# Routed experts taken by size in four lanes, two tables between parts of the shared expert, and the router as paired 64-column products

## The reference, cut to what matters

```python
scores = jax.nn.sigmoid((uf @ w_router).astype(jnp.float32))       # 512 tokens x 64 experts
choice = scores + router_bias.astype(jnp.float32)
...
_, top_e = lax.top_k(masked, TOP_K)                                # 8 experts of each token
wts = wts / jnp.sum(wts, axis=-1, keepdims=True) * ROUTED_SCALE
...
hid = jax.nn.silu(xb @ we_gate[e]) * (xb @ we_up[e])               # 1024 -> 256, twice
return (hid @ we_down[e]) * ws[:, None]                            # 256 -> 1024
...
shared = (jax.nn.silu(uf @ ws_gate) * (uf @ ws_up)) @ ws_down
return (routed + shared).reshape(Bsz, S, D)
```

## Time and profile before

| | us |
|---|---|
| median of the three runs | 2282.85 |
| lowest, highest | 2280.35, 2285.98 |
| the profiled execution, its own time | 2279.11 |
| its span in the trace | 2277.0 |
| routed experts: first product of block 0 to first product of block 47 | 1637.25 to 2232.43 |

### The profile page before, as it was taken

The page is one execution under the profiler, slowest core; times in us unless marked ns, Lnnn a source line. Parts: engine busy times, 40 slices in busy tenths (PEclk is TensorE's granted clock), DMA queues, the critical chain, the costliest instruction groups (busy, mean ns, idle before and its releaser), DMA issues.

```text
span 2277.0 us, 31363 instructions
## 1 busy us (share of the span) xinstructions
PE 2165.5 (95%) x11892; PEld 1561.1 (69%) x11893; DVE 1188.7 (52%) x1772; ACT 720.2 (32%) x1121; POOL 714.3 (31%) x444
## 2 busy tenths in 40 slices
PE   7999999999999999999999999999999999988995
PEld 5867567788778766777777778876555555555553
DVE  6566654998871447789888563245411211211112
ACT  4335654333332343433443345123111111111112
POOL 4331023443353323333333326431122222222220
PEclk9999899999999999999999999999999999999998
DMA  4220132455532223222222213321888889989854
GB/s 160 86 81 2 65 112 74 148 187 182 196 128 95 72 77 93 85 64 75 75 69 62 74 56 111 115 94 74 310 255 286 290 275 322 355 291 375 274 174 127
DMA packets 160062, 344.29 MB, mean 151 GB/s; under 512 B 11457, under 2 KB 100545, under 8 KB 141921
## 3 DMA queue, kind: packets, MB, share of 16 engines
q1 hardware_dynamic: 142496, 297.71, 37.1%
q0 software_dynamic: 15232, 39.02, 7.0%
q10 hardware_dynamic: 2240, 6.29, 0.7%
HBM read 326.19 MB, written 33.55 MB: 158 GB/s over the span
## 4 chain that ended last, share of the span: by engine, by line
PE 81%; DVE 7%; DMA 6%; ACT 2%; issue 2%; SPq 0%; POOL 0%; ACTq 0%; DVEq 0%; POOLq 0%
PE bank L884 24%; PE bank L1566 13%; PE bank L1270 9%; PE bank L1587 7%; PE bank L1191 5%; PE bank L1361 3%; PE bank L875 2%; DMA arena<-in_we_gate 2%; DMA arena<-in_we_down 2%; PE bank L1010 1%; PE bank L1368 1%; DMA arena<-in_w_up 1%; PE bank L893 1%; PE bank L1545 1%; PE bank L1047 1%
## 5 line engine op out<-in xcount | busy, mean ns | idle before, releaser
L1566 PE MATMUL bank<-arena,hn 128*64 128x256 f32 x3072 | 346.4, 384 | 17.5 <-DMA arena<-in_we_gate 15.4
L1566 PEld LDWEIGHTS bank<-arena,hn 128*64 128x64 f32 x3072 | 233.0, 139 | 143.5 <-issue 46.7
L784 POOL TENSOR_TENSOR w_low_flat<-arena,in_high 128x1024 fp32r<-128x1024 f32 (+1 forms) x73 | 186.0, 2569 | 337.1 <-ACT in_high L1892 337.0
L2802 DVE TENSOR_TENSOR inv<-inv,bank 128x256 f32<-128x256 f32 x48 | 20.2, 421 | 332.3 <-PE bank L1566 332.3
L1587 PE MATMUL bank<-arena 128*64 128x512 f32 x768 | 175.4, 598 | 8.0 <-DVE arena L2807 7.9
L1270 PE MATMUL bank<-in_x,in_high 128*128 128x512 f32 x384 | 154.7, 403 | 0.0
L762 POOL TENSOR_TENSOR w_low<-arena,w_high 128x2048 fp32r<-128x2048 f32 x22 | 103.1, 4688 | 161.7 <-ACT w_high L1802 161.7
L1270 PE MATMUL bank<-in_x,w_low_flat 128*128 128x512 f32 x384 | 151.3, 394 | 0.0
L1270 PE MATMUL bank<-x_low,in_high 128*128 128x512 f32 x384 | 151.0, 393 | 0.0
L2814 DVE SCALAR_TENSOR_TENSOR sq<-bank,arena 128x512 f32<-128x512 f32 x96 | 72.1, 751 | 147.8 <-PE bank L1587 145.6
L884 PE MATMUL bank<-x_high,w_high 128*128 128x512 f32 x336 | 133.5, 397 | 1.9 <-POOL w_low L762 1.9
(11 more groups left out here) (479 smaller groups left out, 4883.8 us busy)
## 6 DMA issues: line engine op xcount, KB each, us to landing
arena<-in_we_gate SPq DMA_DIRECT2D x47, 1024.0 KB
arena<-in_we_up SPq DMA_DIRECT2D x47, 1024.0 KB
arena<-in_we_down SPq DMA_DIRECT2D x47, 1024.0 KB
arena<-in_w_in SPq DMA_DIRECT2D x38, 1024.0 KB, 5.4
arena<-in_w_ada SPq DMA_DIRECT2D x12, 2048.0 KB, 8.1
arena<-in_w_up SPq DMA_DIRECT2D x22, 1024.0 KB, 10.8
arena<-in_w_in SPq DMA_DIRECT2D x17, 512.0 KB, 5.2
arena<-in_w_out SPq DMA_DIRECT2D x4, 2048.0 KB, 10.6
```

The costliest lines, as they stand in the source:

```text
L784: pool_eng.tensor_tensor(in2_tile(j, "low"), in2_tile(j, "whole"), in2_tile(j, "high").bitcast(f32), ALU.subtract).then_inc(S("w_low"), 1)
L1566: ins = nc.tensor.matmul(rows_of(banks[2 + part][:, 0:FE], c), columns_of(moe["xT"][:, p, :], k, c), moe["gu"][:, 2 * p + c, at:at + FE], ...
```

## The change

There are four edits.

1. **Router as pairs.** Each of the 8 products of 512 columns becomes two of 256 columns, which write partitions 0 to 63 and 64 to 127 of the same bank. The sigmoid then works on 128x256 instead of 64x512, and two transposes of 128x128 take the place of four.
2. **Experts by size.** Each expert gets the key 64 x halves - number. DVE makes a 64x64 matrix of "has a larger key" times halves, and PE sums it (`ranks`), which gives each expert's start `bstart` with the largest first. The running sum falls away. The expert of a place is found by two comparisons and a product with the numbers 0 to 63. Lanes 0, 1, 2, 3 take fourths 0, 3, 1, 2, so that even blocks pair the largest experts with the smallest.
3. **Tables between the shared expert's parts.** `shared_up(1)` is cut by `ranks`, `shared_down` is cut into residual and halves, and the order of PE's program changes: the first two tables stand ahead of the shared expert's tile 2, the other two between tiles 2 and 3.
4. **The end.** `last_h` runs one tile further ahead, and `last_inverse` stands before `last_out`.

```diff
-                ins = nc.tensor.matmul(banks[0][0:E, :], w[:, k, :], hn[:, k, :], start=k == 0, stop=k == KD - 1)
+                for half in range(2):
+                    ins = nc.tensor.matmul(banks[0][E * half:E * half + E, 0:T // 2], w[:, k, :],
+                                           hn[:, k, T // 2 * half:T // 2 * (half + 1)], start=k == 0, stop=k == KD - 1)
...
-                    if tt == 2 and f == 0:
+                    if tt == 3 and f == 0:
...
+            def ranks():
+
+                pe.wait_ge(S("keys_made"), 1)
+                nc.tensor.matmul(banks[3][:, (TT + 2) * E:(TT + 3) * E], ones[0:E, :], pcol("order")[0:E, 0:E], start=True,
+                                 stop=True).then_inc(S("pe_made"), 1)
...
-            shared_up(1)
+            shared_up(1, 0, 4)
+            ranks()
+            shared_up(1, 4, KD)
+            shared_transposes(0)
+            shared_residual(0)
             run_counts()
-            shared_transposes(0)
+            shared_down(0, 0)
             plan_in_rows()
-            shared_down(0)
+            shared_down(0, 1)
+            shared_transposes(1)
+            shared_residual(1)
+            shared_down(1)
             shared_up(2)
-            shared_transposes(1)
-            shared_down(1)
             shared_up(3)
-            for tt in range(TT):
+            for tt in (0, 1):
                 table(tt)
+            shared_transposes(2)
+            shared_residual(2)
+            shared_down(2)
             for tt in (2, 3):
-                shared_transposes(tt)
-                shared_down(tt)
+                table(tt)
+            shared_transposes(3)
+            shared_residual(3)
+            shared_down(3)
...
+            step(nc.vector.scalar_tensor_tensor(pcol("quarter"), pcol("back"), pcol("key"), pcol("quarter"), ALU.mult, ALU.add))
...
-            step(nc.vector.tensor_tensor_scan(moe["bend"], ones[:, 0:E], moe["nb"], 0.0, ALU.mult, ALU.add))
-            step(nc.vector.tensor_tensor(pcol("bstart"), moe["bend"], moe["nb"], ALU.subtract))
+            keys, own = moe["bend"], pcol("junk")
+            step(nc.vector.scalar_tensor_tensor(keys, moe["nb"], float(E), iota[:, 0:E], ALU.mult, ALU.subtract))
+            for name, of in (("own_key", keys), ("own_halves", moe["nb"])):
+                step(nc.vector.tensor_tensor_reduce(out=own[0:E, :], in0=of[0:E, :], in1=ident[0:E, 0:E], scale=1.0, scalar=0.0,
+                                                    op0=ALU.mult, op1=ALU.add, accum_out=pcol(name)[0:E, :]))
+            nc.vector.tensor_scalar(pcol("order")[0:E, 0:E], keys[0:E, :], pcol("own_key")[0:E, :], pcol("own_halves")[0:E, :],
+                                    ALU.is_lt, ALU.mult).then_inc(S("keys_made"), 1)
...
-            for name, at in (("expert", "half"), ("last", "back")):
-                step(nc.vector.tensor_scalar(pcol("junk"), moe["bend"], pcol(at), None, ALU.is_le, ALU.add,
-                                             accum_out=pcol(name)))
-            for name in ("expert", "last"):
-                step(nc.vector.tensor_scalar(pcol(name), pcol(name), float(E - 1), None, ALU.min))
+            inside = (("expert", "half", pcol("junk")), ("last", "back", pcol("order")[:, 0:E]))
+            for _, at, found in inside:
+                counted_step(nc.vector.tensor_scalar(found, pcol("bstart"), pcol(at), None, ALU.is_le))
+            steps_done()
+            for _, at, found in inside:
+                counted_step(nc.vector.scalar_tensor_tensor(found, moe["bend"], pcol(at), found, ALU.is_gt, ALU.mult))
+            steps_done()
+            for name, _, found in inside:
+                counted_step(nc.vector.tensor_tensor_reduce(out=found, in0=found, in1=iota[:, 0:E], scale=1.0, scalar=0.0,
+                                                            op0=ALU.mult, op1=ALU.add, accum_out=pcol(name)))
...
             last_h(0)
+            last_h(1)
             last_inverse(0)
             for tt in range(TT):
-                if tt + 1 < TT:
-                    last_h(tt + 1)
-                last_out(tt)
+                if tt + 2 < TT:
+                    last_h(tt + 2)
                 if tt + 1 < TT:
                     last_inverse(tt + 1)
+                last_out(tt)
```

More of the change, by code:

```diff
@@ L284, in two_blocks @@
         PLAN_COLS, _ = places([(name, 1) for name in ("lane", "pos", "free", "pairs", "minus", "half", "back", "expert", "last",
-                                                      "new", "first", "needed", "key", "fourth", "fourths", "runs")] +
+                                                      "new", "first", "needed", "key", "fourth", "fourths", "runs", "quarter",
+                                                      "own_key", "own_halves")] +
                               [("bstart", E), ("junk", E), ("order", P), ("in1", TT * TOP), ("in2", TT * TOP),
@@ L331, in two_blocks @@
                                                           "tok_done", "g2_row", "scores", "sc_done"))}
-        PE_MADE = {name: n + 1 for n, name in enumerate(("tok_ready", "g2_spread", "sc_ready", "counted", "runs_counted",
+        PE_MADE = {name: n + 1 for n, name in enumerate(("tok_ready", "g2_spread", "sc_ready", "counted", "ranked", "runs_counted",
                                                          "plan_in_rows"))}
@@ L1421, in score_transposes @@
                 pe.wait_ge(S("act_made"), ACT_MADE["scores"])
-                for tt in range(TT):
-                    ins = nc.tensor.transpose(banks[2][:, tt * E:(tt + 1) * E], SCORES_T[:, tt * P:(tt + 1) * P],
-                                              ident[0:E, 0:E])
+                for q in range(TT // 2):
+                    ins = nc.tensor.transpose(banks[2][:, q * P:(q + 1) * P], SCORES_T[:, q * P:(q + 1) * P], ident)
                 ins.then_inc(S("pe_made"), 1)
@@ L1436, in row_transposes, with shared_up @@
                     ins.then_inc(S("ut_ready"), 1)
-            def shared_up(tt):
+            def shared_up(tt, k0=0, k1=KD):
                 if tt >= 2:
                     pe.wait_ge(S("sh_up"), tt - 1)
-                product(banks[tt % 2][:, :], lambda k: hn[:, k, tt * P:(tt + 1) * P], lambda k: moe["sgu"][:, k, :],
-                        KD).then_inc(S("sh_gu"), 1)
+                for k in range(k0, k1):
+                    ins = nc.tensor.matmul(banks[tt % 2][:, :], hn[:, k, tt * P:(tt + 1) * P], moe["sgu"][:, k, :],
+                                           start=k == 0, stop=k == KD - 1)
+                if k1 == KD:
+                    ins.then_inc(S("sh_gu"), 1)
             def shared_transposes(tt):
@@ L1467, in shared_down @@
                                          h[:, 4 * half + q, tt * P:(tt + 1) * P], ident, start=q == 0, stop=False)
+            def shared_down(tt, *halves):
                 pe.wait_ge(S("sh_hT"), tt + 1)
                 pe.wait_ge(S("down_gated"), 2)
-                for half in range(2):
+                for half in halves or range(2):
                     for k in range(2):
@@ L2084, in _ @@
             act.wait_ge(S("product"), PRODUCTS["router"] + 1)
[L2085 removed]
+            nc.scalar.activation(SCORES_T, banks[0][:, 0:T // 2], ACT.Sigmoid).then_inc(S("act_made"), 1)
             def row_tiles(tt):
@@ L2099, in _ @@
             act.wait_ge(S("ch_done"), 1)
-            nc.scalar.activation(moe["sc"], banks[2][:, 0:TT * E].rearrange("p (t e) -> p t e", e=E), ACT.Copy)\
+            nc.scalar.activation(moe["sc"].rearrange("p (h q) e -> p h q e", h=2), SCORES, ACT.Copy)\
               .then_inc(S("act_made"), 1)
```

37 lines of the change are left out of this document (22 added, 15 removed).

## The result

The median is 2263.62 us (2261.2 to 2269.35, 4 runs) against 2282.26 us before, a ratio of 0.992 with a 95% interval of 0.9897 to 0.9943. Measured again, the same code took 2264.25 us against 2280.58 (0.9929, 0.9914 to 0.9945). The main cause is an edit that the text ahead of the prediction does not list.

The account below looks back on a forecast made before the run. PE, busy 95% of the span, was taken as the bound, with late gate weights stalling the loop. Terms -3.8 + 2.0 - 6.1 + 0.5 = -7.4 us took 2282.85 to 2275.4 us, range 2265 to 2283.

Parts of the forecast that it names:

- The sum of -7.4 us: Whole kernel: -3.8 for block 0's earlier start, +2.0 for its slow clock, -6.1 in the loop, +0.5 at the end.
- The router: Router on PE: paired 256-column products run side by side, so it ends at 1562.9 and not 1566.45, -3.6 us.
- The serial rival: Router: the products of a pair run one after the other; sum about -4, 2279 us; chance 0.07.
- stretch of low clock: PE around the router: TensorE granted 0.50 until about 1562, covering 6 of the 8 steps at 0.86 us.
- Edit 2 on DVE and the tables: Ahead of block 0: about +2.5 us on DVE, covered; last table 1.2 us earlier; block 0 starts 3.8 us earlier, router included.
- Block 0: First loop block: new idle stretches ahead of it slow its products, charged +2.0 us (0 to 2.8).
- The loop: Blocks 0 to 47: two stalls of 8.3 us, at 16/17 and 40/41, 16.6 in place of 22.7, -6.1 us.
- The extra load of block 44: Late in the loop: expert 0 loaded for no rows, behind a block without loads, at no cost; about 8 in a pair.
- most of it is not seen: Loop: stalls stay near 22 because fuller early blocks put 128-row gathers beside loads; -1.3 us, some 2282; chance 0.2.
- the clean loop: Loop: less traffic beside 16/17 and 40/41, both stalls fall to 2 us or less; -20, 2263 us; chance 0.1.
- the slower rival: Loop: two-load blocks 8, 24, 29 and 32 stall beside single loads too; +21, 2303 us; chance 0.05.
- The end: Behind the loop: `last_h(1)` delays `last_inverse(0)` by 1.1 us, partly won back; +0.5 us (-0.6 to +1.2).

Follow-up runs that it names:

- second profile of after: The changed kernel measured and profiled once more, same code: 2264.25 us, 0.9929 of the kernel before; span 2261.5 us.
- kernel with the filling products alone: Kernel before with only the PARTS line changed, moving two slices of a state-space filling product from a group's second step to its first: 2275.11 us, 0.9975.
- run with the old order: Changed kernel with PE's old program order behind the router (only `ranks` kept between the halves of `shared_up(1)`) and the old end: 2267.02 us, 0.9934.
- number order: Changed kernel with the key cut to the expert's number, so experts are taken by number in the new lanes: 2278.17 us, 0.9991.

## Why the prediction was wrong

**The step that failed is the list of the parts.** The text ahead of the prediction says that there are four edits, and the prediction costs four. There are five. The fifth is worth 7.5 us of the stage in every trace that has it. The sum of -7.4 us holds for the four: with these alone the time falls by 6.5 us, 0.9971 (0.9961 to 0.9981). It is not a wrong price but a missing term. I looked for what can be late in the last third of the trace only, and called PE "busy 95% of the span" where 8 waits of up to 0.85 us stood in the middle, each behind filling products that the diff touches.

**The router: right in size, -3.6 forecast, -3.3 and -3.4 measured.** Pairs do run side by side: 6.65 us in place of 9.62, and 5.1 to 6.6 in eight traces with pairs, against 9.1 to 9.9 in five without. The serial rival falls. The stage from its first product on shows only 3.0 us of it, and from line 956 to the transposes of the rows it is even less, 12.4 us before and 10.3 now, since the 2.07 us of that line took 1.16 before. But a cut at the router misleads, because stretches of low clock stand in different places in the two traces. "To rows" in the table begins ahead of all of them: 268.8 to 269.0 us in the five traces without pairs, 265.4 to 265.6 in six with them, and 264.2 in two. The timeline of PE 54 us ahead of the router, and the stretch behind that wait (us, busy time, clock, DMA share, GB/s), before:

```profile
1502.70 0.47 PE L893 MATMUL bank<-mixed_high,late_w_high 128*128 128x512 f32 x1 [2.61 <-ACT mixed_high L2072]
...
1503.00:1507.00 4.00, 4.00 (x13) 2.86 (x12) 4.00 (x1) 3.20 (x7) 3.71 (x1) 0.62 0.95 296
...
1553.99 1.16 PE L954 MATMUL bank<-shp,small 128*128 128x128 f32 x8 [0.64 <-DVE small L2208]
```

The same place in the second profile of after:

```profile
1494.57 0.47 PE L895 MATMUL bank<-mixed_high,late_w_high 128*128 128x512 f32 x1 [2.61 <-ACT mixed_high L2096]
...
1495.00:1499.00 4.00, 4.00 (x18) 2.54 (x17) 4.00 (x1) 3.07 (x6) 3.59 (x1) 1.00 0.99 300
...
1544.57 2.08 PE L956 MATMUL bank<-shp,small 128*128 128x128 f32 x8 [0.64 <-DVE small L2232]
```

Before, the clock fell behind the wait of 2.61 us. After, it did not fall behind the same wait, and the way up to the line ahead of the router is 1.3 us shorter for it. Then it fell sooner ahead of the router, which costs about as much again. The kernel with the filling products alone has both halves of this without any pairs: 1.3 us less up to line 954, 1.3 more from there to the transposes (13.7 us), and 268.9 in all. The forecast held the stretch of low clock fixed, up to 1562, and it isn't fixed: that the price comes so near is in part luck, as the two traces with 264.2 show, in which the same router gave 4.8 us. In the second profile of after the clock is at 0.51 from 1544 us on, 4.3 us ahead of the router, and in the kernel before it is still 0.90 in the 4 us that end 0.8 us ahead of it. The granted clock there (us, busy time, clock, DMA share, GB/s), before:

```profile
1552.00:1556.00 4.00, 2.51 (x21) 2.23 (x20) 0.99 (x3) 1.27 (x4) 1.23 (x1) 0.90 0.00 0
1556.00:1560.00 4.00, 3.17 (x4) 0.98 (x5) 4.00 (x7) 4.00 (x7) 3.44 (x2) 0.50 0.00 0
```

The second profile of after:

```profile
1544.00:1548.00 4.00, 2.08 (x8) 1.78 (x8) 1.49 (x3) 1.74 (x4) 2.65 (x2) 0.51 0.00 0
1548.00:1552.00 4.00, 3.67 (x18) 2.31 (x20) 4.00 (x8) 4.00 (x7) 2.03 (x1) 0.50 0.00 0
```

**Edit 2 on DVE and the tables: right in sum.** "I take nothing" for DVE's longer plan holds, because the new order covers it. Without this order the stage is 1.8 us longer than before. The cut for `ranks` costs 0.6 us where I took 0.1, and the old wait of 0.6 ahead of `plan_in_rows` is gone. Table 0 starts 46.4 us behind the transposes of the rows (1607.50 less 1561.07), as before (1612.87 less 1566.38, 46.5). The gather is where the step was short. POOL issues it 2.8 us behind the last table's end at 1620.2, as expected, and PE waits 3.68 us for it, not 2.7: it lands 6.3 us behind its issue (1629.36 less 1623.07), where I took 5.3. On the other side the wait for ACT is 0.69 us in place of 2.07. In sum block 0 starts 70.9 us behind the transposes, before and after (70.6 in the second profile), where the forecast had -0.2 (its -3.8 without the router's -3.6).

The gather on POOL, after (compare):

```profile
1623.07 1.11 POOL L823 DMA_INDIRECT hn<-u_rows,rows_in  x1 [0.92 <-POOL rows_in L820]
```

**Block 0: +2.0 forecast and 1.8 and 2.0 measured, but this is luck.** I put it on the new idle stretch of 2.7 us. The run with the old order has only the old idle stretches and is slow just the same, and so is the kernel with the filling products alone, whose program there is that of the kernel before. So the 2 us can't be put down to the new order. What decides whether the clock falls is more than the length of the idle times ahead of the block. The Trainium skill (TensorE: Matmul & The Clock Gate, section "Part 1: The HAM clock gate (the "warmup" mystery)") has activity as what releases the clock. Blocks with the same idle times ahead and different clocks show that these rows alone can't predict it. What else differs was not settled: block 0 was fast in three of the four kernels with the old plan and the old order of PE, and slow in all nine traces with the experts by size or the new order of PE.

**The loop: right.** Stalls stand ahead of blocks 17 and 41, beside 0.5 us at block 24 in the first profile. With the slow block behind each they cost 8.0 and 7.7 us, where 2 x 8.3 was forecast. Without block 0 the loop's part is -6.5 us, and -6.8 in the second profile (22.7 to 15.9), in place of -6.1. The extra load of block 44 costs nothing. The rival "most of it is not seen" (stalls near 22), the clean loop and the slower rival fall. The runs with other orders and lanes show the rule as well: two loads behind two cost 5 to 10 us with the slow block behind (12 for the three in a row of the number order). Two beside one cost nothing in both orders by size. In the number order such a group did (3.2 us at block 16, behind 2 and 1), and in the kernel before block 29 was 3.1 us late ahead of its pair, so the rule is not complete. The sum of bytes gives the place but not the size. The rate in the two stretches was 366 and 368 GB/s and not 387, and by that 12.2 million bytes are 33.2 us against a room of 29.5, not the 6 us of the wait.

**The end: right in sign.** +0.5 forecast, about +1 by the mean of the traces.

**The sum by stages**, second profile of after against before: state space -7.5, to rows -3.4, plan -0.3, loop -6.8, block 0 +2.0, end +1.0. With 0.7 ahead of the state-space stage this is the spans' -15.5, but for rounding. The five terms of the listed edits are -7.5, where the forecast had -7.4. The medians' 16.3 to 18.6 lie above the spans' difference by as much as 3 us, and that remainder stays open.

## What to carry to other kernels

Tick off every hunk of the diff against the list of parts before working out the first price, a line of constants above all: a table of slices is as much an edit as a new function. Waits below 1 us that come 8 times are a term of the sum when the diff touches what stands ahead of the wait, and a filler can be shifted from a step with slack into one without at no cost. Before an edit is priced from a stage of two traces, look at the granted clock ahead of it: where a stretch of low clock has moved, measure from a point ahead of both. And times of single-edit runs need not add up: here -5.5 and -6.5 stand beside -16.3, and part of the gap is a slow block that every one of these kernels had once.

## What was not expected of the hardware

The same idle times ahead of the same block in the same program, 1.59, 1.1 and 2.07 us, came with 7.13 us for its products in the kernel before and with 8.81 in the one with the filling products alone. In the same way a wait of 2.61 us at 1500 us was followed by a granted clock of 0.62 in one trace and of 1.00 in the other. The fall of the clock ahead of the router moves by more than a microsecond against the program from kernel to kernel, and its return moves too, so that the paired router takes anything from 5.1 to 6.6 us. And the number order stalled by 3 us at block 16 without a pair of two-load blocks, as the kernel before did at 29 before its pair was complete; what makes a looser group late was not settled.
